# One transformer block with attention, mLSTM and product-key experts: gathered rows handed from VectorE to GpSimd and ScalarE, low parts of U handed to VectorE

## The reference

```python
mod = c @ w_mod + b_mod                              # shift, scale, gate, twice
h = rmsnorm(x, g_pre_mix) * (1 + scale1) + shift1
proj = h @ w_in                                      # attention q, k, v and mLSTM q, k, v, gates
mix = concat([att, mh]) @ w_out                      # windowed attention beside a chunked mLSTM
x = x + gate1 * rmsnorm(mix, g_post_mix)
h2 = rmsnorm(x, g_pre_ffn) * (1 + scale2) + shift2

q = (h2 @ w_q)                                       # 8 heads, two halves of 128
s1, s2 = q_half1 @ keys1.T, q_half2 @ keys2.T        # 128 keys each
# top 16 of each half, the 256 sums of pairs, the top 16 of those -> 16 of 16384 experts a head
gate = softmax(top)
act = gelu(sum(u[eidx] * h2)) * gate                 # u, v: 16384 rows of 1024
y = sum(act * v[eidx])
x = x + gate2 * rmsnorm(y, g_post_ffn)
```

## Time and profile before

| what | us |
|---|---|
| median of 3 runs | 1568.58 (1568.05 to 1570.5) |
| the profiled execution, its own time | 1572.56 |
| its span, first to last instruction | 1570.6 |
| busy: PE | 1514.1 (96%) |
| busy: DVE | 1401.8 (89%) |
| busy: ACT | 595.5 (38%) |
| busy: POOL | 496.5 (32%) |

### The profile page before, as it was taken

The page is one execution under the profiler, slowest core; times in us unless marked ns, Lnnn a source line. Parts: engine busy times, 40 slices in busy tenths (PEclk is TensorE's granted clock), DMA queues, the critical chain, the costliest instruction groups (busy, mean ns, idle before and its releaser), DMA issues.

```text
span 1570.6 us, 23211 instructions
## 1 busy us (share of the span) xinstructions
PE 1514.1 (96%) x8378; PEld 1280.2 (82%) x8378; DVE 1401.8 (89%) x2985; ACT 595.5 (38%) x968; POOL 496.5 (32%) x422
## 2 busy tenths in 40 slices
PE   6999999899999999999999999999999999999997
PEld 4455654688889999999898999989999889787885
DVE  5887886699999999995999999999999999998997
ACT  3103431521555445543333333333333333444343
POOL 1000000232010411010555575555555555343330
PEclk9999999999999999999999999999999999999999
DMA  9764232221454788789999999999999999999993
GB/s 325 267 233 148 89 137 70 66 93 58 134 208 146 269 256 255 249 280 318 396 389 393 408 397 409 402 372 409 408 405 398 382 395 360 368 401 395 398 392 126
DMA packets 180426, 455.71 MB, mean 290 GB/s; under 512 B 15004, under 2 KB 81684, under 8 KB 178136
## 3 DMA queue, kind: packets, MB, share of 16 engines
q1 hardware_dynamic: 113456, 231.84, 41.1%
q0 software_dynamic: 57632, 209.78, 34.7%
q10 hardware_dynamic: 9224, 12.62, 2.4%
HBM read 421.63 MB, written 32.25 MB: 289 GB/s over the span
## 4 chain that ended last, share of the span: by engine, by line
PE 54%; DVE 13%; DMA 4%; issue 2%; ACT 1%; DVEq 0%; ACTq 0%; POOL 0%; POOLq 0%
PE peer_psum L1639 14%; PE peer_psum L1643 7%; PE peer_psum L1699 6%; PE peer_psum L1706 6%; PE peer_psum L1714 6%; PE peer_psum L1651 4%; PE peer_psum L1686 3%; PE peer_psum L1703 3%; PE peer_psum L1709 3%; DMA hT<-in_peer_v,eidx 2%; DVE s_all L1790 2%; DMA s_all<-in_peer_v 2%; PE peer_psum L1624 2%; DVE s_all L1885 1%; DVE s_in L1889 1%
## 5 line engine op out<-in xcount | busy, mean ns | idle before, releaser
L1639 PE MATMUL peer_psum<-hH,hi_slots 128*128 128x320 f32 x1024 | 308.5, 315 | 7.6 <-ACT hi_slots L1582 3.7
L1639 PE MATMUL peer_psum<-hL,hi_slots 128*128 128x320 f32 x1024 | 303.0, 310 | 0.3 <-issue 0.3
L1510 POOL DMA_INDIRECT hT<-in_peer_u,eidx x128 | 149.7, 1169 | 292.1 <-DVE dots L1781 249.4
L1546 ACT ACTIVATE hi_slots<-s_all 128x1024 fp32r<-128x1024 f32 x128 | 135.8, 1061 | 182.0 <-PE peer_psum L1714 169.8
L1639 PEld LDWEIGHTS peer_psum<-hH,hi_slots 128*128 128x128 f32 x1024 | 193.3, 189 | 13.6 <-issue 9.3
L1510 POOL DMA_INDIRECT hT<-in_peer_v,eidx x128 | 146.9, 1148 | 179.5 <-DVE s_all L1790 166.7
L1639 PEld LDWEIGHTS peer_psum<-hL,hi_slots 128*128 128x128 f32 x1024 | 193.4, 189 | 2.8
L1643 PE MATMUL peer_psum<-hH,lo_slots 128*128 128x320 f32 x1024 | 171.9, 310 | 1.5 <-DVE lo_slots L1828 1.5
L1918 DVE TENSOR_TENSOR lo_slots<-s_all,hi_slots 128x1024 fp32r<-128x1024 f32 x128 | 156.3, 1221 | 14.8 <-ACT hi_slots L1546 14.4
L1790 DVE SCALAR_TENSOR_TENSOR s_all<-hT,coef,s_all 128x1024 f32<-128x1024 f32 x126 | 161.1, 1279 | 5.7 <-DMA hT<-in_peer_v,eidx 5.6
L1781 DVE CUSTOM_DVE_ANT_0 hT<-hT,lot 128x1024 f32<-128x1024 f32 x128 | 156.0, 1220 | 6.2 <-DMA hT<-in_peer_u,eidx 4.9
(11 more groups left out here) (317 smaller groups left out, 2853.3 us busy)
## 6 DMA issues: line engine op xcount, KB each, us to landing
ring<-in_peer_u SPq DMA_DIRECT2D x128, 512.0 KB
s_all<-in_peer_v SPq DMA_DIRECT2D x128, 512.0 KB
gate_table<-lot SPq DMA_DIRECT2D x16, 1280.0 KB, 7.1
lot<-gate_table SPq DMA_DIRECT2D x16, 1280.0 KB
gelu_table<-s_all ACTq DMA_DIRECT2D x56, 160.0 KB
s_in<-gelu_table SPq DMA_DIRECT2D x56, 160.0 KB
x_sb<-in_w_mod POOLq DMA_DIRECT2D x8, 1024.0 KB, 7.9
lot<-in_peer_wq SPq DMA_DIRECT2D x8, 1024.0 KB, 5.5
```

Source lines behind the costliest of these rows:

```text
L1510: pool.indirect_dma_start(rows_of(j), None, A[table][0], bass.IndirectOffsetOnAxis(eidx[:, k:k + 1], 0)).then_inc(rows_in[j % RG], 16)
L1546: func(H[:, slot_of(w), :], vb[:, w % RING, :], ACT.Copy).then_inc(v_hi, 1)
L1639: mm(ps[:, bank, 0:TD], H[:, b, c * P:(c + 1) * P], h[:, c, T0:T], start=(c == 0 and h is hH), stop=False)
```

## The change

Four edits. The first two and the last cut pieces smaller or fill PE's waits; the third moves work between engines.

1. mix_block: 14 turns of the identity ahead of PE's wait for the first modulation, and 12 ahead of the first product with `w_in`.
2. query_block: DVE rounds and lowers the first weight slab in two halves of 128x1024; the second half is rounded after the first half's low part. PE waits for the first half alone in query(0).
3. peer_block: the 34 gathered rows of the lead are multiplied by `h_rows` on POOL in place, and summed by ACT with a Copy that has an accumulator output, at the end of ACT's turn, ahead of its store of the GELU. POOL multiplies row j, waits until ACT has summed it, fetches row j + 6, and goes on to row j + 1. POOL's first six fetches stand ahead of its wait for the second `eidx_ready`, its first multiplication behind it. DVE's planner has no rows in the lead. `LOW_BY_DVE` becomes every block from 18 on, so blocks 18 to 24 and 35 to 39 move from PE and ACT to DVE.
4. The last tile of the output is finished and stored in two halves of 128x512.

```diff
-LOW_BY_DVE = [n for n in range(LEAD) if 25 <= n < 35 or n >= 40]
+LOW_BY_DVE = [n for n in range(LEAD) if n >= 18]
+BY_POOL = sum(ROWS_LEAD)
...
                 bk.wait_free(pe, "modc", s, h)
+                if (s, h) == ("first", 0):
+                    turn_ident(14, "modc", s, h)
...
                     mod_columns("first", 0)
+                    turn_ident(12, "mq", 0)
...
-            v.tensor_copy(wqH[:, 0, :, :], wq[:, 0, :, :]).then_inc(wq_hi_first, 1)
+            v.tensor_copy(wqH[:, 0, :, 0:P], wq[:, 0, :, 0:P]).then_inc(wq_hi_first, 1)
...
-            dve.wait_ge(wq_hi_first, 1)
-            v.tensor_tensor(wqL[:, 0, :, :], wq[:, 0, :, :], wqH[:, 0, :, :].bitcast(F32), ALU.subtract).then_inc(wq_lo_first, 1)
+            for m in range(2):
+                part = slice(m * P, m * P + P)
+                if m:
+                    v.tensor_copy(wqH[:, 0, :, part], wq[:, 0, :, part]).then_inc(wq_hi_first, 1)
+                dve.wait_ge(wq_hi_first, m + 1)
+                v.tensor_tensor(wqL[:, 0, :, part], wq[:, 0, :, part], wqH[:, 0, :, part].bitcast(F32), ALU.subtract).then_inc(wq_lo_first, 1)
...
+            for j in range(RG):
+                fetch(j)
+            pool.wait_ge(eidx_ready, 2)
+            pool.dma_start(eidx[NB:P, K:K + KB], chosen_u[0:NB, 0, KB:K]).then_inc(eidx_b_in, 16)
+            for j in range(BY_POOL):
+                pool.wait_ge(rows_in[j % RG], 16 * (j // RG + 1))
+                nc.gpsimd.tensor_tensor(rows_of(j), rows_of(j), h_rows, ALU.mult).then_inc(pool_made, 1)
+                fetch(j + RG)
+            for j in range(BY_POOL + RG, NROWS):
+                fetch(j)
...
                 for m in STEPS[it]:
                     stage_gates(m)
+                for j in range(BY_POOL):
+                    if TURN_OF[j] == it:
+                        act.wait_ge(pool_made, j + 2)
+                        func(rows_of(j), rows_of(j), ACT.Copy, accum_out=dots[:, j:j + 1]).then_inc(row_done, 1)
                 act.wait_ge(s_ready, it + 1)
                 act.dma_start(S_dram[it], act_out[:, it % 2, :]).then_inc(s_stored[it % 2], 16)
...
-                for _ in range(ROWS_AT[it]):
-                    take_row()
-                    clock += 1.14
...
-                v.scalar_tensor_tensor(out=y[:, t, :], in0=y[:, t, :], scalar=stat[:, 1, i:i + 1], in1=x_sb[:, t, :],
-                                       op0=ALU.mult, op1=ALU.add).then_inc(out_ready, 1)
+                for at in ((slice(0, D),) if i < 3 else (slice(0, 512), slice(512, D))):
+                    v.scalar_tensor_tensor(out=y[:, t, at], in0=y[:, t, at], scalar=stat[:, 1, i:i + 1], in1=x_sb[:, t, at],
+                                           op0=ALU.mult, op1=ALU.add).then_inc(out_ready, 1)
```

More of the change, by code:

```diff
@@ L81 @@
 STEPS_OF = {1: NB // GT, 2: P // GT, 3: P // GT}
-EIDX_B_AT = RG
 LATE = 2
@@ L1238, in query_block @@
             sem(n) for n in ("h_hi", "h_lo", "wq_hi", "wq_hi_first", "wq_lo", "wq_lo_first", "q_top_chain"))
-        wait_wq_lo = lambda eng, s: eng.wait_ge(wq_lo, s) if s else eng.wait_ge(wq_lo_first, 1)
-        wait_wq_hi = lambda eng, s: eng.wait_ge(wq_hi, s) if s else eng.wait_ge(wq_hi_first, 1)
+        wait_wq_lo = lambda eng, s: eng.wait_ge(wq_lo, s) if s else eng.wait_ge(wq_lo_first, 2)
+        wait_wq_hi = lambda eng, s: eng.wait_ge(wq_hi, s) if s else eng.wait_ge(wq_hi_first, 2)
         block = ctx.enter_context(nc.Block())
@@ L1314, in query @@
                         nc.tensor.transpose(bk("q", m)[:, 0:P], keep["ident"][:], keep["ident"][:])
-                wait_wq_hi(pe, s)
+                if m == 0:
+                    pe.wait_ge(wq_hi_first, 1)
+                else:
+                    wait_wq_hi(pe, s)
                 at = slice((m % 2) * P, (m % 2) * P + P)
@@ L1322, in query @@
                         mm(bk("q", m), wqH[:, s % 2, c, at], h[:, c, :], start=(c == 0 and h is hH), stop=False)
-                wait_wq_lo(pe, s)
+                if m == 0:
+                    pe.wait_ge(wq_lo_first, 1)
+                else:
+                    wait_wq_lo(pe, s)
                 for c in range(DC):
@@ L1400, in peer_block @@
         u_in, v_in, s_loaded, out_done = keep["u_in"], sems("v_in", RING), sems("s_loaded", RING), sems("out_done", NT)
-        (iota_ready, consts, chain, top_ready, gate_exp, sel_ready, selT_full, selT_done, hot_dve, g_full,
+        (pool_made, consts, chain, top_ready, gate_exp, sel_ready, selT_full, selT_done, hot_dve, g_full,
          g_staged, eidx_ready, eidx_b_in, hb_in, row_done, dots_gelu, coef_ready) = (sem(n) for n in (
-             "iota_ready", "peer_consts", "x_dve_chain", "top_ready", "gate_exp", "sel_ready", "selT_full", "selT_done", "hot_dve",
+             "pool_made", "peer_consts", "x_dve_chain", "top_ready", "gate_exp", "sel_ready", "selT_full", "selT_done", "hot_dve",
              "g_full", "g_staged", "eidx_ready", "eidx_b_in", "hb_in", "row_done", "dots_gelu",
@@ L1485, in _, with fetch @@
                     sp.dma_start(out[0, 0:P, :], y[:, 0, :]).then_inc(out_done[0], 16)
-            for i, t in enumerate(TILES[1:]):
+            for i, t in enumerate(TILES[1:3]):
                 sp.wait_ge(out_ready, i + 2)
                 sp.dma_start(out[0, t * P:(t + 1) * P, :], y[:, t, :]).then_inc(out_done[t], 16)
+            t = TILES[3]
+            for h in range(2):
+                sp.wait_ge(out_ready, 4 + h)
+                sp.dma_start(out[0, t * P:(t + 1) * P, h * 512:(h + 1) * 512], y[:, t, h * 512:(h + 1) * 512]).then_inc(out_done[t], 16)
             for t in range(NT):
-                sp.wait_ge(out_done[t], 16)
+                sp.wait_ge(out_done[t], 32 if t == TILES[3] else 16)
         @block.gpsimd
         def _(pool):
-            nc.gpsimd.iota(iota_i[:], pattern=[[1, P]], base=0, channel_multiplier=0).then_inc(iota_ready, 1)
+            nc.gpsimd.iota(iota_i[:], pattern=[[1, P]], base=0, channel_multiplier=0).then_inc(pool_made, 1)
             pool.wait_ge(eidx_ready, 1)
-            for j in range(NROWS):
-                if j == EIDX_B_AT:
-                    pool.wait_ge(eidx_ready, 2)
-                    pool.dma_start(eidx[NB:P, K:K + KB], chosen_u[0:NB, 0, KB:K]).then_inc(eidx_b_in, 16)
+            def fetch(j):
                 if j == K:
@@ L1749, in _ @@
             step = Chain(dve, chain)
-            dve.wait_ge(iota_ready, 1)
+            dve.wait_ge(pool_made, 1)
             step(v.tensor_copy(iota[:], iota_i[:]))
@@ L1758, in _ @@
             step(v.tensor_tensor(fold[:, 2 * NB:3 * NB], pairs[:, :, 0], pairs[:, :, 1], ALU.add))
-            rows_taken = 0
+            rows_taken = BY_POOL
             def take_row():
@@ L1765, in take_row @@
                 rows_taken += 1
+                if j == BY_POOL:
+                    dve.wait_ge(row_done, BY_POOL)
                 if j == K:
```

## The result

The changed kernel takes 1629.28 us (median of 4 runs, 1626.02 to 1634.13), the kernel before 1569.53 beside it (4 runs). The ratio is 1.038, with a 95% interval from 1.0363 to 1.0398: slower by 57 to 62 us. The forecast was 1610 with a range of 1580 to 1626. The direction is right, the time lies above the range.

What follows compares the result with a forecast made beforehand. PE and DVE were taken to bound the lead. 22.2 + 1.0 + 4.0 + 0.4 + 10.7 + 7.2 - 2.1 - 1.4 - 0.5 = +41.5 on 1572.6 gave 1614.1, forecast as 1610 because that execution lay 4.0 above the median; range 1580 to 1626.

Steps and rivals of the forecast that it cites:

- The stall: Turn 18: PE waits for block 18's low part, queued behind tile 3 on DVE; +22.2 us, and +1.0 for low clock.
- The holding inside tiles 2 and 3: Ahead of turn 18: POOL's first multiplications delay DVE by 2.0, 1.0 and 1.0 us; +4.0, bounds 0 and 9.2.
- The loss per row: Lead: each POOL multiplication of 2.35 us takes 2.0 from DVE, bounds 0 and 2.3.
- By the rule the sum is the one I use: Lead: with the port lock also holding tensor_scalars such as L1821, the sum stands with its 2.0 us a row.
- Rival 2: Lead: the stall comes and POOL holds only two-input operations, about 1.0 us a row; +20.8, or 1589 us; chance 0.18.
- Rival 1: Lead: the stall comes, but POOL takes nothing from DVE; +12.6, or 1581 us; chance 0.17.
- rival 3: Turn 18: DVE's low part is there when PE asks, so no stall; -15.7, or 1553 us; chance 0.04.
- Rival 4: Lead: POOL's multiplication is nearer 3.5 us, or low clock returns in many short waits; 25 more, or 1635; chance 0.12.
- Turns 18 to 26: Lead: POOL's closed loop of about 4.95 us a turn eats PE's gain; 44.3 against 43.9, +0.4 us.
- Turns 27 to 39: Lead: DVE's queue with 12 losses of 2.0 decides; 120.7 against 110.0, +10.7 us.
- PE needs about 102.0: Turns 27 to 39 before the change: of 110.0 us PE needs about 102.0, and DVE set the rest.
- Both ends: Start -2.1 us, query_block -1.4, last store -0.5, from smaller pieces and filled waits.

Runs made afterwards that it cites:

- the repetition: The changed kernel, unedited, profiled a second time: 1625.1 us in one run.
- Experiment 2: The changed kernel with the lead's 34 rows given back to DVE, its low parts from block 18 on kept: 1595.2 us, ratio 1.0154.
- Experiment 3: The changed kernel with `LOW_BY_DVE` as before the change, rows staying with POOL and ACT: 1598.01 us, ratio 1.0186.
- experiment 4: The changed kernel without POOL's multiplication by `h_rows`; fetches, ACT's sums and low parts stay: 1582.23 us, ratio 1.0087.
- experiments 5 and 6: The changed kernel with POOL's multiplication over 512 of 1024 columns, then with a copy of h in its place: 1600.28 and 1596.36 us.
- experiment 1: The kernel before with only the pieces at both ends of the change, rows and low parts as before: 1567.66 us, ratio 0.9998.

## Why the prediction missed

**The stall: right in its mechanism, and lucky in its number.** +27.4 against 22.2 + 1.0 + 4.0 = 27.2, released by DVE's L1860 as written. But GELU(18) came 29.4 later than before (526.06 against 496.65): 22.2 by the order of the queue, 6.5 by the holding, 1.1 by the low clock and 0.2 left over, less 0.6 because DVE was early. PE was itself 2.0 late at GELU(17), and that alone brings 29.4 down to 27.4. In the repetition the stretch is 33.2 longer than before. Within it the low clock cost 2.50 - 1.44 = 1.1 in turn 18 and 0.5 in turn 19 (4.92 for 4.40), 1.6 for my 1.0. Experiment 2 has the stall with rows by VectorE and 3 has none, so it is the edit on `LOW_BY_DVE` alone. The holding inside tiles 2 and 3 was 6.5, not 4.0 (experiment 4): the first multiplication met a tensor_scalar and took some 2.6 from DVE instead of 2.0, the third another and some 2.9 instead of 1.0. Ahead of it DVE was 0.6 early (432.12 for 432.70 at the end of tile 0).

**The loss per row: the step that failed.** "2.35 would take 1.97; I use 2.0 a row, with 0 and 2.3 as bounds." It is 2.84, above the upper bound. The mechanism was the right one: L1853 is held, L1860 isn't, and the hold lasts as long as POOL's operation. The size of this one term makes 6.7 of the miss in turns 27 to 39, 5.0 in turns 40 to 50, and part of the 2.5 inside tiles 2 and 3. I took the price from the earlier trace rows, where POOL's L428 of 0.63 took only 0.25 from DVE. There one long DVE operation met it and both engines were slowed. Experiment 3 shows that case again: a tensor_tensor of 1.83 begins 0.84 ahead of the multiplication and keeps its time, and the multiplication takes 3.24 instead of 2.39. Timelines of DVE and POOL:

```profile
510.08 1.83 DVE L1916 TENSOR_TENSOR s_all<-s_all,s_in 128x1600 f32<-128x1600 f32 x1
```

```profile
510.92 3.24 POOL L1534 TENSOR_TENSOR hT<-hT,lot 128x1024 f32<-128x1024 f32 x1
```

In the gate rows DVE has a queue of short operations without a gap instead: one of them waits for all of POOL's operation, and 0.43 to 0.46 comes on top whatever the length (experiments 5 and 6). The upper bound should have been POOL's duration and something, not less than the duration. That it is the queue that makes the difference is my reading of these rows; no run varied it by itself.

A turn with three steps follows to the hundredth: 1.14 + 4.89 + 2.84 = 8.87, and it took 8.86. I had 8.03. Six of the eleven turns from GELU(40) to GELU(51) take 8.84 to 8.86, which makes 5.0 of the 5.3 that are missing there.

The Trainium skill (SBUF — State Buffer, Who interferes with whom) says that VectorE and GpSimd share a pair of ports as an exclusive lock, which whoever issues first holds for the whole instruction, and that a tensor_scalar in a two-port mode contends for it too. The runs agree: 2.84 for 2.38 at a tensor_scalar. "By the rule the sum is the one I use" was wrong, though: a lock for the whole instruction takes at least the multiplication's 2.35 out of a full queue, by estimate, and the sum had 2.0.

Rival 2 (only the two-input operations held) is excluded by L1853. Rival 1 (no holding) falls with the same rows, rival 3 with the stall. Rival 4's time, 1635, is nearest to the result, but for another reason: it had a multiplication of 3.5 us, which took 2.39, and the low clock in many short waits. PE waited 29 times for one-hot rows between GELU(27) and GELU(40), and the lower clock followed one of these waits (571 us, on the way to GELU(28)).

**Turns 18 to 26: -2.7 for +0.4.** "The gain on PE is eaten by this loop." It closes in 4.85 as forecast (multiplications at 533.72 and 538.57), but PE ran at 4.40 all the same and used up the turn made ahead and ScalarE's slack. The delay came out in one piece, in turn 26 with 6.28, and half of it isn't the loop's: without the multiplication (experiment 4) that turn takes 5.32. The whole stretch takes 41.2 with it and 41.0 without it.

**Turns 27 to 39: +22.1 for +10.7.** From GELU(28) to GELU(32) each turn took what it took before, since DVE had slack for the holds (it waits 0.63 and 1.26 us for ScalarE's high parts there). The eight turns from GELU(32) to GELU(40) took 92.0, where the kernel before takes 66.6 + 8.5 = 75.0. 0.84 x 8 = 6.7 of that is the error in the hold: a turn of four steps is 1.14 + 4 x 1.63 + 2.84 = 10.50 and took 10.48, one of five is 12.13 and took 12.10 to 12.13. My sum had 84.8 for these eight, so 7.2 of the missing 11.4 lie there. The other 4.1 lie in the five turns from GELU(27) to GELU(32), 40.1 against a forecast of 36.0, and come from one of them, that from GELU(27) to GELU(28) (4.9 more than forecast; the rest took 0.8 less). It shows how a hold reaches PE at once. Timelines of DVE and PE:

```profile
567.37 3.90 DVE L1853 TENSOR_SCALAR s_all<-iota,lot 128x128 f32<-128x128 f32 x4
571.19 1.21 DVE L1860 TENSOR_TENSOR lo_slots<-peer_psum,hi_slots 128x1024 fp32r<-128x1024 f32 x1
```

```profile
571.33 2.08 PE L1681 MATMUL peer_psum<-s_all 128*128 128x128 f32 x8 [3.27 <-DVE s_all L1853]
573.20 1.80 PE L1654 MATMUL peer_psum<-ident,ring 128*128 128x128 f32 x8
```

PE has no stock of one-hot rows at the first gates, waits 3.27, and does the next 16 products at half the clock. The turn takes 11.30, where it took 6.18 before and I had 6.4. And "PE needs about 102.0" was 107.0 (experiment 4), which would have made rival 1 about 4 us dearer. So "DVE set the rest" was wrong too: of the 110.0 before, PE waits 1.4 for DVE's one-hot rows.

**Both ends: -4.0 forecast, +2.6 came.** The +2.2 at GELU(0) is PE's. DVE, which sets GELU(18), was 0.6 early, so on the path through the stall the ends are worth -0.6 instead of -3.5. At the start the twelve products took what was forecast (the earlier trace rows had 8.28 for them):

```profile
25.24 5.39 PE L490 MATMUL mix_psum<-hT,slab 128*128 128x512 f32 x12 [0.17 <-issue]
32.81 1.02 PE L463 MATMUL mix_psum<-ones,mod_sum 128*128 128x1 f32 x8 [2.18 <-DVE mod_sum L888]
```

But DVE began the second modulation at 26.66, having waited 1.52 for its weights, so -0.7 was left of -2.1. In the seven other profiles with these edits they weren't late, and -1.9 to -2.3 came (the repetition has -2.0). The lower clock took it back at 206 and 397. The halves in the query block gave the 1.4 that were forecast: the offset to the kernel before goes from +0.7 at 212 us to -0.7 at 304 in experiment 1, and from -2.0 to -3.5 in the repetition. The last store cost 0.4 instead of giving 0.5: from PE's last product to the end it is 12.0 to 12.2 in all eight profiles with it, and 11.7 or 11.9 in the five without. DVE's four operations take 3.81 from first to last where the three took 3.68, one more issue follows, and a half lands 3.3 to 3.4 us after its issue, a whole one 2.6 to 3.2.

**After the lead: -5.8, not forecast.** DVE waits less for gathered rows there, 5.9 us instead of 12.3; but the repetition waits 8.9 and gains more, 6.5. The kernels in which POOL has a part in the lead's rows, or ScalarE alone sums them, gain 3.6 to 6.5 between GELU(56) and the last products against the profile of before. The others lie between +1.6 and -4.8. The two sets overlap. Whether it is the rows' work or chance stays open.

## What to carry to other kernels

Before work is handed to GpSimd, count what it takes from VectorE. Where VectorE's queue was full of short tensor_scalars, each GpSimd operation cost it that operation's duration and nearly half a microsecond; here up to 2.84 us to save a fused row of 1.15. It was free beside the subtractions that read PSUM and beside the searches.

A planner that emits one engine's queue must know each waiter's due time. An operation of 1.2 us that was left behind 30 us of other work cost 27. And a gain that was read off a stretch at the lower clock is to be doubted until a second stretch can be excluded.

## What the runs showed of the hardware

- GpSimd operations of 1.04 us (copy), 1.28 (multiplication of 512 columns) and 2.38 (of 1024) each made the VectorE tensor_scalar beside them longer by their duration and 0.43 to 0.49, where its queue was full.
- Not held were a subtraction with one input in PSUM (1.22 beside GpSimd, 1.23 alone) and the searches (0.08 and 0.20). GpSimd's own multiplication took 2.35 to 2.44, but 2.91, 3.23 and 3.24 where a tensor_tensor of VectorE with both inputs in SBUF (1.50 to 1.83) had begun 0.84 ahead of it (experiment 3).
- After 26.57 us in which it waited, TensorE's products ran at the lower of its clock levels for the first 2.50 us. Ahead of GELU(28) a wait of 3.27 was followed by it, too.
- All thirteen profiles lose 3.3 to 5.1 us to the lower clock in the first 405 us. Where they lose it differs from kernel to kernel, and in the changed kernel from one execution to the next.
- In six of thirteen profiles ScalarE stands still for 4.5 to 6.0 us in turn 7 of the lead. The kernel before has it in one of two executions, the changed one too.
